# Another order of the eight expert passes in a mixture-of-experts layer

## The reference

```python
logits = (xt @ router_w).astype(jnp.float32)
top_vals, top_idx = lax.top_k(logits, TOP_K)            # TOP_K = 2 of N_EXPERTS = 8
top_p = jax.nn.softmax(top_vals, axis=-1)
gates = jnp.sum(jax.nn.one_hot(top_idx, N_EXPERTS, dtype=jnp.float32) * top_p[..., None], axis=1)
out = jnp.zeros_like(xt)
for e in range(N_EXPERTS):
    out = out + gates[:, e:e + 1] * swiglu(xt, w13[e], w2[e])   # w13 1024 x 7168, w2 3584 x 1024
```

## Time and profile before

| | before |
|---|---|
| runs | 1332.7, 1333.49, 1335.66 us, median 1333.49 |
| profiled execution: its time | 1335.29 us |
| its span, first to last instruction | 1333.4 us (1.9 us lie around it) |
| TensorE matmul busy | 1310.0 us, 98% of the span |
| VectorE, ScalarE busy | 407.2 and 333.2 us |
| DMA | 444.27 MB, 333 GB/s over the span |
| mean granted TensorE clock | 0.998 |

### The profile page before, as it was taken

The page is one execution under the profiler, slowest core; times in us unless marked ns, Lnnn a source line. Parts: engine busy times, 40 slices in busy tenths (PEclk is TensorE's granted clock), DMA queues, the critical chain, the costliest instruction groups (busy, mean ns, idle before and its releaser), DMA issues.

```text
span 1333.4 us, 24932 instructions
## 1 busy us (share of the span) xinstructions
PE 1310.0 (98%) x10817; PEld 857.9 (64%) x10817; DVE 407.2 (31%) x778; ACT 333.2 (25%) x629; POOL 14.8 (1%) x28
## 2 busy tenths in 40 slices
PE   9999999999999999998999999999999999999987
PEld 6989888888798986432667666335666335666322
DVE  6686754444748765000111100101100201100201
ACT  6565554443646642000001000001000001000002
POOL 1100000000000000000000000000000000000000
PEclk9999999999999999999999999999999999999999
DMA  8936255454543689999999999999999999999995
GB/s 320 334 131 227 95 186 187 186 188 185 187 178 120 248 342 372 398 423 421 420 420 421 419 409 404 410 420 421 420 420 420 421 420 421 419 420 420 421 421 232
DMA packets 64057, 444.27 MB, mean 333 GB/s; under 512 B 7309, under 2 KB 8733, under 8 KB 11208
## 3 DMA queue, kind: packets, MB, share of 16 engines
q1 hardware_dynamic: 61976, 436.96, 81.3%
q0 software_dynamic: 1824, 5.42, 1.2%
q10 hardware_dynamic: 144, 0.26, 0.1%
HBM read 441.17 MB, written 1.44 MB: 332 GB/s over the span
## 4 chain that ended last, share of the span: by engine, by line
PE 92%; DMA 4%; DVE 2%; SPq 1%; ACT 1%; issue 0%; DVEq 0%; ACTq 0%
PE up_banks L2259 34%; PE bank L2259 17%; PE bank L1759 7%; PE bank L1761 7%; PE bank L1760 7%; DMA raw<-in_moe_units 4%; PE up_banks L1759 3%; PE up_banks L1761 3%; PE up_banks L1760 3%; PE bank L2323 1%; PE bank L2206 1%; PE bank L1854 1%; SPq L536 1%; PE bank L2236 1%; PE bank L1801 1%; DVE w_lo L1060 1%
## 5 line engine op out<-in xcount | busy, mean ns | idle before, releaser
L1651 DVE TENSOR_TENSOR hidden<-hidden,up_banks 128x384 f32<-128x384 f32 (+1 forms) x56 | 27.3, 487 | 583.3 <-ACT hidden L992 583.3
L1060 DVE TENSOR_TENSOR w_lo<-raw,w_hi 128x1024 fp32r<-128x1024 f32 x154 | 181.5, 1219 | 42.3 <-ACT w_hi L665 40.9
L665 ACT ACTIVATE w_hi<-raw 128x1024 fp32r<-128x1024 f32 x154 | 155.1, 1057 | 47.7 <-PE bank L1761 39.6
L992 ACT ACTIVATE hidden<-up_banks 128x384 f32<-128x384 f32 (+1 forms) x56 | 24.5, 437 | 476.6 <-PE up_banks L2259 476.6
L2259 PE MATMUL up_banks<-raw,mid_x 128*32 128x256 f32 (+1 forms) x1260 | 95.0, 450 | 0.0
L2259 PE MATMUL bank<-raw,hT 128*32 128x256 f32 (+2 forms) x716 | 82.0, 486 | 2.3 <-DMA raw<-in_moe_units 2.2
L1759 PE MATMUL bank<-xT_hi,w_hi 128*128 128x256 f32 x288 | 82.5, 287 | 0.0
L1760 PE MATMUL bank<-xT_lo,w_hi 128*128 128x256 f32 x288 | 81.5, 283 | 0.0
L1761 PE MATMUL bank<-xT_hi,w_lo 128*128 128x256 f32 x288 | 81.4, 283 | 0.0
L2259 PEld LDWEIGHTS up_banks<-raw,mid_x 128*32 128x32 f32 x1260 | 57.3, 110 | 33.3 <-issue 1.6
L983 ACT ACTIVATE hT<-bank 128x384 f32<-128x384 f32 (+1 forms) x56 | 24.4, 437 | 208.4 <-PE bank L2323 208.4
(11 more groups left out here) (421 smaller groups left out, 2099.9 us busy)
## 6 DMA issues: line engine op xcount, KB each, us to landing
raw<-in_moe_units SPq DMA_DIRECT2D x108, 1024.0 KB, 23.5
slot_w_hi<-in_moe_units SPq DMA_DIRECT2D x46, 1024.0 KB, 24.8
slot_w_lo<-in_moe_units SPq DMA_DIRECT2D x46, 1024.0 KB, 25.1
raw<-in_layer_units SPq DMA_DIRECT2D x44, 1024.0 KB, 4.9
raw<-in_dense_units SPq DMA_DIRECT2D x33, 1024.0 KB, 4.8
slot_bias<-in_moe_units SPq DMA_DIRECT2D x19, 1024.0 KB, 22.5
slot_xT_lo<-in_moe_units SPq DMA_DIRECT2D x18, 1024.0 KB, 23.1
slot_xT_hi<-in_moe_units SPq DMA_DIRECT2D x18, 1024.0 KB, 23.0
```

The source lines that it names most:

```text
L665: act.activation(w_hi[:, st.split(u), half, :], raw[:, st.slot(u), half * n:(half + 1) * n], ACT.Copy)\
L992: act.activation(hidden_of(n), ups_of(n, 1), ACT.Silu).then_inc(sem("silu"), 1)
L1060: dve.tensor_tensor(w_lo[:, st.split(u), half, :], raw[:, st.slot(u), half * n:(half + 1) * n], w_hi[:, st.split(u), half, :].bitcast(F32) ...
L1651: dve.tensor_tensor(hidden_of(n), hidden_of(n), ups_of(n, 0), ALU.mult)\
```

## The change

The order of the items becomes M0 S1 M0 S2 M3 S4 M5 M6 S7. As before, four items are M and four are S, and items 0, 1, 6 and 7 keep their kind and their rank. Two M items now follow each other as sixth and seventh (M5, M6), and after the rest of M0 comes an S item. A table says which item is M, another which rank of expert goes to which item, and a third which two columns a `gather_pair` serves. With the ranks taken from a table, four small VectorE instructions of `experts_by_count` go away and the comparison that makes `who` moves up. The pair gathers stay at the end of the odd items.

```diff
+MANY = (True, False, False, True, False, True, True, False)
+RANK_OF_ITEM = (7, 0, 1, 4, 2, 5, 6, 3)
+PAIRED = ((3, 2), (5, 4), (6, 7))
...
-            many = i % 2 == 0
+            many = MANY[i]
...
             c.step(dve.tensor_scalar(is_few, rank_e, float(FEW_RANKS - 1), None, ALU.is_le))
-            c.step(dve.tensor_scalar(place_e, rank_e, 2.0, -6.0 - NE, ALU.mult, ALU.add))
-            c.step(dve.tensor_scalar(rank_e, rank_e, float(NE - 1), float(-NE), ALU.is_equal, ALU.mult))
+            c.step(dve.tensor_tensor(who[:, 0:NE, :], by_other(rank_e), by_own(less8[:, 1, :]), ALU.is_equal))
             c.wait()
             c.step(dve.tensor_scalar(cap, is_few, float(FEW - MID), float(MID), ALU.mult, ALU.add))
-            c.step(dve.scalar_tensor_tensor(place_e, is_few, float(NE - 1), place_e, ALU.mult, ALU.add))
             c.wait()
             c.step(dve.tensor_tensor(chunks, total, cap, ALU.is_gt))
             c.step(dve.tensor_scalar(past, cap, float(MID), None, ALU.add))
-            c.step(dve.tensor_tensor(place_e, place_e, rank_e, ALU.add))
             c.wait()
             c.step(dve.tensor_tensor(past, total, past, ALU.is_gt))
-            c.step(dve.tensor_tensor(who[:, 0:NE, :], by_other(place_e), by_own(less8[:, 0, :]), ALU.is_equal))
...
-                for a, rows, col in ((0, MID, 2 * n + 2), (MID, FEW, 2 * n + 3)):
+                for a, rows, col in zip((0, MID), (MID, FEW), PAIRED[n]):
...
-                    back(i - 1, i == 2 or not many, (0, 1), spread, y_hi, y_lo)
+                    back(i - 1, i == 2 or MANY[i - 1], (0, 1), spread, y_hi, y_lo)
...
-                elif j == ITEM_STEPS and not many:
+                elif j == ITEM_STEPS and i % 2:
                     gather_pair(i // 2)
```

More of the change, by code:

```diff
@@ L97, in shape_constants @@
     mats[:, 3, :] = np.arange(P)[None, :]
-    less8 = np.tile(np.arange(NE, dtype=np.float32) - NE, (P, NT, 1))
+    less8 = np.tile(np.stack([np.arange(NE) - NE, np.array(RANK_OF_ITEM)]).astype(np.float32), (P, 1, 1))
     at = np.arange(P, dtype=np.float32)
@@ L397, in _build @@
     info = sb("info", [1, 1 + ITEMS], I32)
-    sizes = sb("sizes", [P, 10, NE])
+    sizes = sb("sizes", [P, 9, NE])
     who = sb("who", [P, ITEMS, NE])
@@ L421, in _build @@
     fewer, level_e = above[:, 0, :, :], level[:, 0, :, :]
-    counted, rank_e, is_few, cap, place_e, total, chunks, past, turn_of, turn_end = (sizes[:, n, :] for n in range(10))
+    counted, rank_e, is_few, cap, total, chunks, past, turn_of, turn_end = (sizes[:, n, :] for n in range(9))
     place8 = pool_b[:, 1, 0:NT * NE].rearrange("p (t e) -> p t e", t=NT)
@@ L1013, in _ @@
             if i < NE - 1:
-                if not many:
+                if i % 2:
                     pair_in(i // 2)
@@ L2394, in between @@
                     pe.wait_ge(sem("spread"), i)
-                    back(i - 1, i == 2 or not many, (0, 1), spread, y_hi, y_lo)
+                    back(i - 1, i == 2 or MANY[i - 1], (0, 1), spread, y_hi, y_lo)
                 elif j == 2:
-                    back(i - 1, i == 2 or not many, (2, 3), spread, y_hi, y_lo)
+                    back(i - 1, i == 2 or MANY[i - 1], (2, 3), spread, y_hi, y_lo)
                 elif j == 3:
```

## The result

The change is slower by 0.16%: 1336.34 us (median of 18 runs) against 1334.41 us (18 runs), ratio 1.0016 with a 95% interval of 1.0009 to 1.0022. The profiled execution of the changed kernel took 1335.7 us with a span of 1333.9 us, the one of before 1335.29 and 1333.4.

The account below looks back on a forecast made before the run. Loads were taken to set the end up to load 328, with TensorE's lag held by 20 buffers; after the change, TensorE from load 211. 8.0 late less 6.6 of waits gives +1.4; 1333.49 + 1.4 + 0.4 = 1335.3 us, range 1332.3 to 1338.0.

Parts of the forecast that it names:

- What bounds the kernel: Loads 62 to 328 set the end, 672.3 us for 266 units; TensorE needs the rest from there.
- The items' costs from the parts of other items: TensorE's time per reordered item: S2 and S4 78.8 us, M3 and M5 119.9, M6 116.2.
- The lag: TensorE behind the loads: 31.4 us at item 2, dry in S4 (8.1 us wait), item 7 8.0 late, no waits there.
- 3.05 us of loading lost: Dip in GB/s at 780 to 860 us, from a full ring; the change gets these 3.05 us back.
- the net of +1.4 us: Item 7 starts 8.0 us later, but its 6.6 us of waits for loads vanish.
- a correction of +0.4 for the median: Half of 0.8 us given back if quicker loads made the median 1.8 us lower than the profiled execution.
- VectorE at 0: Four fewer ranking instructions, some 0.3 us, taken as 0; a gain of 0.3 us at most.
- the boundary M5 to M6 at 0: Pair copies between items 5 and 6 have 7.3 us of slack: 0 us, at most 1.
- B: Rival, slower: the 780 to 860 us dip isn't the full ring's, loads come no sooner; +4.5, 1338.0 us; chance 0.20.
- C: Rival, faster: loads still set the end, 3.05 us won and nothing lost, 1330.4 us; chance 0.05.
- D: Rival, nothing moves: loads set the pace in every item, M items too; 1333.5 us; chance 0.07.
- the case that I had held likeliest: Time of the whole kernel within 0.2% (2.7 us) of before; chance 0.66.

Follow-up runs that it names:

- the gather experiments: One pair gather done twice: changed kernel's item 5, 1340.26 us; kernel before's item 5, 1334.77; changed kernel's item 3, 1336.05; all against 1334.17 us.
- experiment 3: Order M0 S1 M0 M2 S3 S4 M5 M6 S7, first half as before, second as in the change: 1336.77 against 1334.67 us of the kernel before.
- experiment 2: Order M0 S1 M0 S2 M3 M4 S5 M6 S7, against the kernel before: 1333.34 against 1334.67 us, repeated 1333.23 against 1334.69.
- experiment 5: Loads of items 2 to 7 wait for four more reads: kernel before 1343.7, changed 1337.31, both against 1333.74; order S2 M3 M4 S5 1334.05 against 1334.69 us.

## Why the prediction was right, and what in it was wrong

**What bounds the kernel** held: loads up to TensorE's last wait, and the gather experiments show it (4.44 us of work hidden before, with +0.6 us left of it; behind load 211 of the change they bring it from +1.9 to +6.1 us).

**The items' costs from the parts of other items** held to 0.2 us each: S2 78.9 for 78.8, M3 119.9 for 119.9, M5 119.7 for 119.9, M6 116.2 for 116.2. Rearranged work can be priced from rows of before, part by part.

**The lag** held: TensorE dry in S4, item 5 at 1003.74 for 1003.9, item 7 at 1239.66 for 1240.0 (7.7 us late for 8.0), the unit at load 328 at 1302.41 for 1302.7, no wait in item 7. But that the absolute times fit to 0.3 us is partly luck: this execution's loads were 1.15 us early at load 62, and that hid an error of about the same size.

**The error is the term "3.05 us of loading lost".** The dip in the rate was read as time that the loads lose and that the change gives back, and the loads' own pace was put at 2.516 us a unit. It is (1003.60 - 627.84) / 149 = 2.522 where nothing holds it. By the two profiles the change gives back 1.5 us from load 62 to 211, but experiment 3, with a deeper dip than before, loses nothing against the change there; over the nine profiles with the whole ring the dip is worth some 1 us up to load 328. With 2.522, load 211 lands 0.9 us later than I had it, and the net of +1.4 us becomes +2.3; counted from load 62 the profiles show +2.2, and the medians +1.9. So that the forecast difference of +1.8 us (1335.3 against 1333.49) comes so near to the +1.9 is luck in part: it is +1.4, which was too small by this term, and a correction of +0.4 for the median, for which there was a reason but no evidence. No run here shows that correction. The absolute 1335.3 is 1.0 us below the 1336.34 measured, nearly all of it because the median of the kernel before rose from 1333.49 (3 runs) to 1334.41 (18 runs).

**VectorE at 0** and **the boundary M5 to M6 at 0** held. With the shorter ranking load 21, the first that needs `info`, is issued 13.1 us after load 20 instead of 13.4, but load 22 is issued 14.3 us after load 20 in both kernels, so what was gained is gone one load later. The copies of the pair for items 6 and 7 end 7.2 us before TensorE wants them, for 7.3 predicted: at 1116.01 + 0.27 in this row of ScalarE's timeline, with item 6 starting at 1123.44.

```profile
1116.01 0.27 ACT L970 ACTIVATE few_x<-bank 128x128 f32<-128x128 f32 x1
```

**The rivals.** B (the dip isn't the full ring's) is refuted in its cause by experiments 2 and 5 and by the issue times, though half of its consequence is true: little loading came back. Load 211 landed at 1003.60, or at 1004.75 if load 62 is taken at its 628.99 of before, not far short of the 1005.2 from which B would decide. C and D needed a stage that is bound by loads to the end; the change isn't, the order of experiment 2 is. The Trainium skill ("DMA: Bandwidth & Descriptors", Specifications) with its 358 GB/s would have led to D; the 418 to 423 GB/s of the windows outside the dips goes with the other figure of that page, the 425 of its Bandwidth section for one core with the other idle. The advice to interleave (the Trainium skill, "Perfetto Trace Analysis", Optimization Strategy) says nothing of the place, and here the place decides: two M items in a row were free as items 3 and 4 and cost 2 us as items 5 and 6.

The measured +1.9 us lies within 0.2%, the case that I had held likeliest.

## What to carry to other kernels

When a stage is fed by a stream through a ring, keep a ledger: at each item's start, how far the consumer lags behind the loads. In this kernel an order is good if the lag stays above zero and below what the ring holds until the last items, as in experiment 2; heavy items belong where the lag is small and light ones after them, and the last heavy stretch must leave the light items behind it enough time to catch up. Total work and busy share say nothing here: both kernels have 1310.0 us of TensorE.

## What the runs showed of the hardware

A dip in GB/s need not delay the consumer by what the rate says: a dip worth 3 to 4 us cost the loads some 1 us by their last raises, with a single execution for each kernel behind this figure. A load of 1 MB is down in 16 parts, and these don't keep one pace: from load 62 to 211 the first raises of the change are 370.1 us apart and the last ones 375.8, and by load 328 the first part of a unit is down 12.2 us before the last. The rate shows the sum of the parts, the consumer waits for the last one, and a ring that is nearly full takes the lead of the first ones before anything else (at load 144 it is 2.8 us in the kernel before and 4.5 in the change). When the ring was shorter by four buffers, the last raises of the kernel before lost 9.4 us as well.
